# A transformer kernel's opening in another order: x in four loads, sums tile by tile, six modulation vectors by TensorE

## What is computed

```
c_act = jax.nn.silu(c)
for l in range(DEPTH):
    mod = (c_act @ ada_w[l] + ada_b[l])[:, None, :]
    sh1, sc1, g1, sh2, sc2, g2 = jnp.split(mod, N_MOD, axis=-1)
    h = rmsnorm(x, norm1_g[l]) * (1.0 + sc1) + sh1
    x = x + g1 * token_mix(h, w_in[l], w_fourier[l], w_ret[l], w_out[l])
    ...
def rmsnorm(x, g):
    xf = x.astype(jnp.float32)
    y = xf * lax.rsqrt(jnp.mean(xf * xf, axis=-1, keepdims=True) + EPS)
    return (y * g.astype(jnp.float32)).astype(x.dtype)
```

## Time and profile before

| | us |
|---|---|
| median of the runs | 3003.31 |
| lowest, highest (3 runs) | 3002.44, 3006.01 |
| span of the profiled execution | 3002.8 |
| PE busy in it | 2963.0 |
| DVE, ACT, POOL busy | 1785.7, 1128.1, 226.3 |
| first matmul of `several` | 23.96 |
| first matmul behind `several` | 60.89 |

### The profile page before, as it was taken

One profiled execution on the slowest core, in us unless ns is written; L12 is line 12 of the kernel. 1 busy time (PEld: TensorE's weight loads), 2 busy tenths in 40 slices (PEclk: granted clock), 3 DMA queues, 4 the chain that ended last, 5 costly groups with the idle time before them and its releaser, 6 DMA issues. The chain is left out here.

```text
span 3002.8 us, 36219 instructions
## 1 busy us (share of the span) xinstructions
PE 2963.0 (99%) x14767; PEld 2491.8 (83%) x14767; DVE 1785.7 (59%) x2589; ACT 1128.1 (38%) x1690; POOL 226.3 (8%) x184
## 2 busy tenths in 40 slices
PE   7999999999999999999999999999999999999999
PEld 6888888888888888888888899888899866788887
DVE  7767666765867667677757656323357656443233
ACT  4433332433424333333434344222235556332222
POOL 0300000000001201100000011000011014100000
PEclk9999999999999999999999999999999999999999
DMA  7454355344433433344443344232235230123221
GB/s 287 152 183 141 126 182 196 126 141 136 144 126 114 152 120 121 109 148 140 148 136 137 133 134 162 98 99 93 97 126 173 91 126 8 57 92 98 98 97 65
DMA packets 107781, 383.83 MB, mean 128 GB/s; under 512 B 11964, under 2 KB 13372, under 8 KB 107616
## 3 DMA queue, kind: packets, MB, share of 16 engines
q1 hardware_dynamic: 83856, 296.51, 29.5%
q10 hardware_dynamic: 23760, 85.01, 8.7%
HBM read 379.37 MB, written 2.10 MB: 127 GB/s over the span
## 5 line engine op out<-in xcount | busy, mean ns | idle before, releaser
L1888 DVE TENSOR_TENSOR WL<-stage,WH 128x1024 fp32r<-128x1024 f32 x508 | 630.5, 1243 | 563.1 <-ACT WH L1256 562.9
L455 PE MATMUL ps<-HH,WH 128*128 128x512 f32 x2184 | 853.4, 391 | 0.3 <-DVE WL L1888 0.3
L456 PE MATMUL ps<-HL,WH 128*128 128x512 f32 x2184 | 850.2, 389 | 0.0
L457 PE MATMUL ps<-HH,WL 128*128 128x512 f32 x2184 | 849.9, 389 | 0.0
L1256 ACT ACTIVATE WH<-stage 128x1024 fp32r<-128x1024 f32 x512 | 537.6, 1053 | 440.7 <-PE ps L457 429.1
L455 PE MATMUL ps<-GH,WH 128*128 128x512 f32 (+2 forms) x1649 | 572.0, 347 | 2.6 <-DVE SCR L2557 1.8
L456 PE MATMUL ps<-GL,WH 128*128 128x512 f32 (+2 forms) x1649 | 569.0, 345 | 0.0
L457 PE MATMUL ps<-GH,WL 128*128 128x512 f32 (+2 forms) x1649 | 569.0, 345 | 0.0
L457 PEld LDWEIGHTS ps<-HH,WL 128*128 128x128 f32 x2184 | 409.9, 188 | 85.8
L455 PEld LDWEIGHTS ps<-HH,WH 128*128 128x128 f32 x2184 | 410.1, 188 | 83.6 <-issue 1.4
L456 PEld LDWEIGHTS ps<-HL,WH 128*128 128x128 f32 x2184 | 410.2, 188 | 82.7
(11 more groups left out here) (265 smaller groups left out, 2905.1 us busy)
## 6 DMA issues: line engine op xcount, KB each, us to landing
stage<-ws SPq DMA_DIRECT2D x535, 512.0 KB, 3.3
MST<-wm ACTq DMA_DIRECT2D x154, 512.0 KB, 3.3
Z<-wm SPq DMA_DIRECT2D x10, 512.0 KB, 7.9
TAB<-consts ACTq DMA_DIRECT2D x7, 448.0 KB, 3.5
MST<-wm SPq DMA_DIRECT2D x6, 512.0 KB, 7.2
out<-X SPq DMA_DIRECT2D x8, 256.0 KB, 2.2
X<-xT SPq DMA_DIRECT2D x4, 256.0 KB, 5.2
X<-xT ACTq DMA_DIRECT2D x4, 256.0 KB, 5.5
```

What stands on the lines that cost most here:

```text
L455: e.matmul(o, wh, mh, start=start, stop=False, **more)
L456: e.matmul(o, wh, ml, start=False, stop=False, **more)
L457: return e.matmul(o, wl, mh, start=False, stop=stop, **more)
L1888: e.tensor_tensor(wl, src, wh.bitcast(F32), ALU.subtract).then_inc(wlo.sem, wlo.up(("w", i)))
```

## The change

It touches the first 60 us and nothing behind.
- x comes in four loads of 512 KB (two tiles each, 4 KB in a row): loads 0 and 2 from SP, 1 and 3 from ACT. ACT squares tiles 0, 1, 4 and 5 and DVE tiles 2, 3, 6 and 7. Nothing is added up on DVE: PE sums each tile for itself, four one-column matmuls for each of eight tiles (`first_sums`), with single calls of `warm` between.
- Vectors m = 0 to 5 (scale and shift of tiles 0, 1 and 2) move from DVE to PE (`shift_and_scale`): eight one-column matmuls for each, the weights as the stationary operand, a column of silu(c) (CC, a load of 4 KB at the head of ACT's queue) as the moving one. The pair of tile 0 stands behind the sums and ahead of `rms_last`; those of tiles 1 and 2 stand inside `several`, between the 12 and the 6 matmuls of steps 0 and 1. DVE adds the bias from PSUM (two columns). The other ten vectors stay with DVE, two steps ahead of their use instead of one, and both now behind HL.
- SP's queue: PAR is cut in two, its head sooner and its tail late; the first weights stand ahead of modulation tiles 2 to 5, and silu's wide input behind them. The tiles of m = 6 to 11 go into buffers that PE frees.
- ACT splits one chunk of weights ahead of the first HH instead of two, and takes silu of CB behind the second HH.
- POOL does one power instruction at the start, on ones. PE starts with 12 warm matmuls instead of 4.

```diff
+BY_PE = 6
...
         def mod_freed(m):
-            return (ev, "cond", MODS[m][3]) if MODS[m][0] == "cond" else (modv, "m", m)
+            return (mm, "mod", m) if m < BY_PE else (ev, "cond", MODS[m][3]) if MODS[m][0] == "cond" else (modv, "m", m)
...
                         e.matmul(p[:, :], wl, mh, start=False, stop=False)
+                    if norm == ("n1", 0) and 2 * k + 3 < BY_PE:
+                        shift_and_scale(k + 1)
                     pe.wait_ge(lo, "h", norm, k)
...
+            def first_sums():
+                k = ("n1", 0)
+                for i, t in enumerate(SUM_ORDER):
+                    pe.wait_ge(*((sq if t in ACT_SQUARES else ssq), "sq", k, t))
+                    for c in range(4):
+                        inst = e.matmul(STAT[:, c:c + 1], first_square(t)[:, c * 128:c * 128 + 128], OC[:, 0:1],
+                                        start=i == 0 and c == 0, stop=i == 7, skip_group_check=True)
+                    done(inst, ("sum", k, t), *([("ss", k)] if i == 7 else []))
+                    warm(FIRST_WARM[i])
+
+            def shift_and_scale(t):
+                if t == 0:
+                    pe.wait_ge(ev, "ccol")
+                for i, m in enumerate((2 * t + 1, 2 * t)):
+                    b, w = mod_buffer(m)
+                    pe.wait_ge(modl[b], "m", m)
+                    for k in range(8):
+                        inst = e.matmul(PS[7][:, i:i + 1], w[:, k * 128:k * 128 + 128], CC[:, k:k + 1],
+                                        start=i == 0 and k == 0, stop=k == 7, skip_group_check=True)
+                    done(inst, ("mod", m))
...
-                warm(4)
-                rms_first(("n1", l), S, 0, 7)
-                warm(4)
+                if l:
...
+                else:
+                    warm(12)
+                    first_sums()
+                    shift_and_scale(0)
+                    warm(4)
                 rms_last(("n1", l), S, dv, "aff", ("n1", l), 7)
                 warm(4)
...
-                    weights(ahead=AHEAD)
+                    weights(ahead=AHEAD - 1)
...
                     affine_one(k, t, S, hx, lambda t: MOD[:, l, t:t + 1])
+                    if l == 0 and t == 1:
+                        act.wait_ge(cond_in, "cond")
+                        e.activation(CB[:, 0, :], CB[:, 0, :], ACT.Silu).then_inc(ev.sem, ev.up(("silu",)))
...
-                    for t in range(1, 7):
-                        add_square(k, t, S)
+                    for t in DVE_SQUARES:
+                        T = take(("sq", k, t), mm, "sum", k, t)
+                        dve.wait_ge(x_in[t // 2], "x")
+                        e.tensor_tensor(T, X[:, t, :], X[:, t, :], ALU.mult).then_inc(ssq.sem, ssq.up(("sq", k, t)))
+                    rms_first(k, S)
                     dve.wait_ge(par_in, "par")
-                    mod_work(0, 0)
-                    rms_first(k, S)
-                    for m in range(1, 4):
-                        mod_work(m, 0)
...
                     for t in range(DT):
+                        if 2 * t < BY_PE:
+                            dve.wait_ge(mm, "mod", 2 * t)
+                            e.tensor_tensor(MOD[:, 0, t:t + 9:8], PS[7][:, 0:2], PAR[:, PCOLS["adab"] + t:PCOLS["adab"] + t + 9:8],
+                                            ALU.add).then_inc(modv.sem, modv.up(("m", 2 * t), ("m", 2 * t + 1)))
...
                         next(steps)
-                        if 1 < t + 1 < DT:
-                            mod_work(2 * t + 2, 0)
-                        elif t == 0:
+                        if t == 0:
                             weights((k, 0), ahead=0)
                         next(steps)
-                        if 1 < t + 1 < DT:
-                            mod_work(2 * t + 3, 0)
+                        if BY_PE // 2 <= t + 2 < DT:
+                            mod_work(2 * t + 4, 0)
                         weights((k, t), ahead=1)
+                        if BY_PE // 2 <= t + 2 < DT:
+                            mod_work(2 * t + 5, 0)
...
+            pool.wait_ge(dv, "v4")
+            e.tensor_tensor(V4[:, 4:8], V4[:, 0:4], HM[:, :], ALU.pow).then_inc(power.sem, power.up(("one",)))
...
+            for i in (0, 2):
+                e.dma_start(X[:, 2 * i:2 * i + 2, :].rearrange("p a b -> p (a b)"), xT[i]).then_inc(x_in[i].sem, x_in[i].up(("x",)))
+            e.dma_start(PAR[:, 0:128], params[:, 0:128]).then_inc(par_in.sem, par_in.up(("par",)))
+            mod_load(0)
+            mod_load(1)
+            e.dma_start(IDN[:, :], consts[:, 0:128]).then_inc(idn_in.sem, idn_in.up(("idn",)))
+            load(0)
+            mod_load(2)
+            mod_load(3)
+            load(1)
+            mod_load(4)
+            mod_load(5)
             e.dma_start(CB[:, 0, :], cond).then_inc(cond_in.sem, cond_in.up(("cond",)))
...
+        ACT_SQUARES, DVE_SQUARES, SUM_ORDER = (0, 1, 4, 5), (2, 3, 6, 7), (0, 2, 1, 3, 4, 6, 5, 7)
+        FIRST_WARM = (1, 0, 1, 4, 0, 0, 0, 0)
```

More of the change, by code:

```diff
@@ L188, in drain, with program @@
             self.advance()
-def program(nc, ws, wm, xT, cT, params, cond, consts, sel_d, out, plan):
+def program(nc, ws, wm, xT, cT, params, cond, ccol, consts, sel_d, out, plan):
     dry, chunks, upto = plan.dry, plan.chunks, plan.upto
@@ L210, in program @@
         modl = [signal(f"md{i}", 16) for i in range(6)]
-        x_in = [signal(f"x{t}", 16) for t in range(DT)]
+        x_in = [signal(f"x{t}", 16) for t in range(DT // 2)]
+        col_in, par2_in = signal("col", 16), signal("par2", 16)
         par_in, cond_in, idn_in, dft_in, c_in, rope_in, sel_in, mask_in, stored = (
@@ L1611, in swiglu @@
                         square(("ao", {"c": 0, "x": 0, "y": 2}[who], 1 if who == "c" else 0), nn, zt(nn), n, first=nn == 0)
[L1613 to L1620, removed]
+            e.dma_start(CC[:, :], ccol).then_inc(col_in.sem, col_in.up(("col",)))
+            for i in (1, 3):
+                e.dma_start(X[:, 2 * i:2 * i + 2, :].rearrange("p a b -> p (a b)"), xT[i]).then_inc(x_in[i].sem, x_in[i].up(("x",)))
+            act.wait_ge(col_in, "col")
+            e.activation(CC[:, :], CC[:, :], ACT.Silu).then_inc(ev.sem, ev.up(("ccol",)))
+            for t in ACT_SQUARES:
+                T = take(("sq", ("n1", 0), t), mm, "sum", ("n1", 0), t) if t else SSQ
+                act.wait_ge(x_in[t // 2], "x")
+                e.activation(T[:, :], X[:, t, :], ACT.Square).then_inc(sq.sem, sq.up(("sq", ("n1", 0), t)))
             token_mix(0)
@@ L1955, in rms_first @@
                 dve.wait_ge(mm, "ss", k)
-                if NORMS.index(k):
-                    dve.wait_ge(power, NORMS[NORMS.index(k) - 1])
+                dve.wait_ge(power, NORMS[NORMS.index(k) - 1] if NORMS.index(k) else "one")
                 sums = DEN if k in TILE_SUMS else STAT
@@ L2830, in load @@
                 e.dma_start(stage[:, i % NS, :], ws[i]).then_inc(landed[i % NS].sem, landed[i % NS].up(("w", i)))
-            for t in range(4):
-                e.dma_start(X[:, t, :], xT[t]).then_inc(x_in[t].sem, x_in[t].up(("x",)))
-            e.dma_start(CB[:, 0, :], cond).then_inc(cond_in.sem, cond_in.up(("cond",)))
[L2835 to L2840, removed]
-            for i in range(1, 6):
-                load(i)
-                mod_load(2 * i + 4)
-                mod_load(2 * i + 5)
+            for i in (0, 2):
+                e.dma_start(X[:, 2 * i:2 * i + 2, :].rearrange("p a b -> p (a b)"), xT[i]).then_inc(x_in[i].sem, x_in[i].up(("x",)))
+            e.dma_start(PAR[:, 0:128], params[:, 0:128]).then_inc(par_in.sem, par_in.up(("par",)))
[8 more added lines that the diff above has]
+            mod_load(5)
+            e.dma_start(CB[:, 0, :], cond).then_inc(cond_in.sem, cond_in.up(("cond",)))
+            for i in range(2, 6):
+                load(i)
+                mod_load(2 * i + 2)
+                mod_load(2 * i + 3)
+            mod_load(14)
+            mod_load(15)
+            e.dma_start(PAR[:, 128:NP], params[:, 128:NP]).then_inc(par2_in.sem, par2_in.up(("par",)))
             e.dma_start(DFTF, consts[:, 128:384]).then_inc(dft_in.sem, dft_in.up(("dft",)))
@@ L2868, in program, with first_square @@
         EARLY = [6, 2]
+        ACT_SQUARES, DVE_SQUARES, SUM_ORDER = (0, 1, 4, 5), (2, 3, 6, 7), (0, 2, 1, 3, 4, 6, 5, 7)
+        FIRST_WARM = (1, 0, 1, 4, 0, 0, 0, 0)
+        def first_square(t):
+            k = ("n1", 0)
+            return (SA("sq", k, t) if t else SSQ) if t in ACT_SQUARES else SD("sq", k, t)
         BESIDE_OG = [2, 3, 4]
@@ L3037 @@
             a = v * 1024 + t * 128
-            wm[i] = src["ada_w" if which == "ada" else "w_mod"][l, :, a:a + 128].T
-    arrays = {"ws": ws, "wm": wm, "xT": A(A(x)[0].T).reshape(8, 128, S), "cT": A(A(ctx_2)[0].T).reshape(8, 128, C),
+            w = src["ada_w" if which == "ada" else "w_mod"][l, :, a:a + 128]
+            wm[i] = w.reshape(8, 128, 128).transpose(1, 0, 2).reshape(128, 1024) if i < BY_PE else w.T
```

(1 more changed line is left out.)

13 lines of the change are left out of this document (10 added, 3 removed).

## The result

| | before | changed |
|---|---|---|
| median of 5 runs, us | 3003.36 | 3024.49 |
| lowest, highest | 3002.44, 3006.01 | 3023.28, 3026.08 |
| span of the profiled execution | 3002.8 | 3021.9 |
| first matmul of `several` | 23.96 | 32.55 |
| first matmul behind `several` | 60.89 | 80.57 |

The changed kernel is 1.0070 times as long, 95% interval 1.0059 to 1.0081: 21 us slower by the medians, 19.1 by the spans. The first matmul behind `several` is 19.7 later, so the whole loss lies in the opening. The page shows TensorE with 2989.7 us of work where it had 2963.0: 26.7 more, for six vectors, six more tiles to sum and 14 more warm matmuls.

What follows compares the result with a forecast made beforehand. TensorE, busy 2963.0 of 3002.8 us, was taken as the bound, so opening delays go through to the end. Start +8.5, steps +10.4 and clock +5.8 sum to 24.7; with 3003.3 that gives 3028 us, range 3009 to 3034.

Steps and rivals of the forecast that it cites:

- rival 1: The clock falls in the opening's sums but holds in `several`: 8.5 + 10.4, 3022 us; chance 0.21.
- The start of `several`: Opening up to `several`: TensorE's slow sums and tile 0's pair delay its start from 23.96 to 32.4, +8.5 us.
- rival 2: Sums and all else run at the high clock throughout: -1.9 + 10.4 = +8.5 us, 3012; chance 0.12.
- The steps of `several`: Seven steps inside `several`, lengthened by pairs on TensorE and DVE's waits: 43.1 us against 32.8, +10.4.
- The chain from the pair to the next first matmul: Steps 0 and 1 of `several`: DVE's bias, AB and aff up to the next first matmul, 2.05 us.
- The wait ahead of HL: Steps 2 to 5 of `several`: DVE, with both vectors behind HL, waits for HH, 0.88 us.
- The clock inside `several`: Half of each pair and half of the next step's 12 matmuls run slow: +5.8 us, bounds 0 and 11.6.
- From span to median: Whole kernel: the timed median was taken as 0.5 us above the span, so 24.7 was added to 3003.3.
- The parts at nothing: Opening and moved loads: x's sooner landing, sooner weights, later silu and POOL's early power were put at zero.

## Why the prediction was right, and where it was off

Forecast 3028, measured 3024.5, inside the range. The range held rival 1 as well, so that it was met whether or not the clock fell inside `several`.

**The start of `several`**, +8.5 forecast, +8.6 measured (32.55 against 23.96). Each of its steps stood: sums from 6.46 (6.3) to 19.90 (19.7), the pair of tile 0 6.83 (6.8), the spread and the split behind it. That the warm ones lift the clock and the sums let it fall was an assumption; the windows show it, and the warm matmuls between every tile show the cause. The Trainium skill, TensorE: Matmul & The Clock Gate, section LDWEIGHTS, with its one figure for a load, would have had rival 2; the loads at 333 ns from 10 us on refute that reading. The kernel with warm matmuls between agrees with the page's 107 ns in the distance of its records, because its clock was held; the loads themselves took 186 ns or more in every row shown.

**The steps of `several`**, +10.4 forecast. Measured from first matmul to first matmul: 8.57, 8.86, 5.52, 4.90, 5.94, 5.94 and 4.21, where 8.2, 8.2, 5.94, 4.81, 5.94, 5.94 and 4.1 stood; the whole of `several` is 48.0 against 36.9, +11.1. The chain from the pair to the next first matmul is 2.21 (38.91 to 41.12), where I wrote 2.05; the terms that I named add up to 1.95. The wait ahead of HL is 0.79, as named. Giving one vector its old place showed the wait by itself: DVE's step becomes 5.06, the 0.88 that I put on it.

**The clock inside `several`**, +5.8 forecast, is the term that was mis-sized. In the profiled execution it cost some 0.3 on the path. I took half of each pair slow by rows 9. But both pairs ran at the high clock (64 loads at 187 to 192 ns), and only 47.6 to 51.0 was slow, behind the second pair. The six HL matmuls of step 1 lasted 2.75 instead of 1.52, and step 2 started at 49.98, 0.3 later than HH alone would have let it (it was ready at 49.51); step 3 waits for ACT's HH (55.50) and so for DVE, which had lost nothing. Rows 9 show a long stretch in which most matmuls were narrow; a pair between 12 and 6 wide ones is 3.5 us. The other half of the term, slow matmuls behind a pair, is real: with one vector between it came behind both pairs, and cost 1.0 ahead of aff of tile 2. So rival 1 (3022) had the sum that came, 8.5 + 10.4 = 18.9 against the span's 19.1, but its clock that holds inside `several` is only half true, and it was partly luck that this profile shows the fall where it costs nothing. The mean granted clock of the five executions is 0.992 to 0.994, the profiled one being among the highest; where the others had their low clock isn't known.

**From span to median.** I added the 0.5 between one execution's span and the median of other runs. The profiled execution of the changed kernel took 3023.98 at a span of 3021.9, and every execution here has 1.8 to 2.2 us outside its span. So before's profiled one took 3004.6 to 3005.0 by estimate, above its median of 3003.36, and the changed kernel's lay under its own; the difference of the medians, 21.1, is 2 more than that of the spans, and the forecast's 24.7 has to be held against either. Rival 1 gives 3022.2 by the same sum, 2.3 too low, mostly for that reason. And 3028 looks closer than its terms were: the 2 us that the medians add hide a part of the clock's 5.8.

**The parts at nothing** were so: x landed at 9.10 and brought nothing with TensorE behind it, the sooner weights alone are no measurable change, and silu behind the second HH held DVE up for 0.20 only (at 41.76), under TensorE's work. POOL's power was shorter, as I wrote, for a reason that I had wrong: not the early one, but DVE idle beside it.

## What to carry to other kernels

Before narrow matmuls are given to an idle TensorE, count their records at both clocks, and ask what stands behind them: here the last 40 of the sums' 64 records and the 32 of a pair behind them cost 0.2 each, with four wide ones in all between them. Putting fillers between holds the clock but takes the time that it saves, and fillers at the low clock are pure delay. Free the tail before its feeders: the four loads and the two squaring engines were worth nothing with eight tiles to sum behind them, and were part of a gain of 3 us with six.

## What was unexpected of the hardware

- 32 one-column records between wide matmuls took 3.48 to 3.59 in the three kernels that have them singly, so the clock held in them, or nearly to their end. Behind them it fell after the second pair here and after both in the kernel with one vector between. 64 in a row brought it to 0.54 within them. Where exactly it falls moves with no change nearby: the sums ended at 19.90 here, at 18.65 and 20.47 in two kernels with the same sums. Why isn't shown.
- In the kernel before, the profile shows a granted clock of 1.00 over an opening in which loads take 333 ns; the changed kernel's shows 0.50 for the like. It too shows 1.00 over its first 5 us, in which its 12 warm matmuls take 0.44 each (1.18 to 6.46), the time of the low level. The durations were right.
- POOL's power took 1.01 with DVE idle and 2.07 or 2.08 beside a vector on DVE (1.99 before), and DVE's add took 1.63 beside POOL's add and 0.69 alone. POOL's add ends at 9.47 (8.09 + 1.38), and DVE's, begun at 8.38, at 10.01, 0.54 behind: one seems to wait for the whole of the other. The Trainium skill, SBUF — State Buffer, section 🔬 SBUF: two separate sides, has it as an exclusive lock on a port pair between GpSimd and a VectorE operation with two SBUF inputs. The rows of the adds agree; those of the power only in part, for DVE's second vector, begun at 15.02, took its usual 1.28 beside the power's last 0.87.
